# A sparse-attention mixer: one product for the compressed scores of both key groups, and keys, copies and low parts put in another order

## What is computed

```python
kc = apply_rope(rms_norm(compress(heads(k_cmp), pe_k, w1_k, w2_k), g_kc), ang_c[:, None])   # 2 groups x 15 keys x 64
vc = compress(heads(v_cmp), pe_v, w1_v, w2_v)
def block_fn(i):                                   # 128 queries at a time, 2 blocks
    m_c = cmp_end[None, :] <= tq[:, None]
    p_c = masked_softmax(jnp.einsum('bhgqd,bhnd->bhgqn', qb, kc) * scale, m_c)
    o_c = jnp.einsum('bhgqn,bhnd->bhgqd', p_c, vc)
    ...                                            # o_s: selected blocks, o_w: window
    return gb[..., 0:1] * o_c + gb[..., 1:2] * o_s + gb[..., 2:3] * o_w
```

## Time and profile before

| | us |
|---|---|
| median of 3 runs (1245.08 to 1246.0) | 1245.83 |
| the profiled execution | 1243.11 |
| its span | 1241.4 |
| PE busy | 1220.3 (98%) |
| DVE busy | 703.9 (57%) |
| ACT busy | 553.9 (45%) |
| mean granted TensorE clock, share of full | 0.99 |

### The profile page before, as it was taken

How to read it: one execution, slowest core, us unless ns; L and a number is a source line. 1 busy time by engine, 2 the same in 40 slices (tenths; PEclk the granted TensorE clock), 3 DMA queues, 4 the chain that set the end, 5 groups by cost and what they waited for, 6 DMA issues and landing times.

```text
span 1241.4 us, 14939 instructions
## 1 busy us (share of the span) xinstructions
PE 1220.3 (98%) x6235; PEld 1022.3 (82%) x6235; DVE 703.9 (57%) x714; ACT 553.9 (45%) x656; POOL 62.5 (5%) x121
## 2 busy tenths in 40 slices
PE   8999999999999999999999999999999997999998
PEld 6888888888889978888888888888888776888886
DVE  5667455455465755555546555546935776555452
ACT  5535344334355534543434534434656233444430
POOL 2100000000010001000000000002200010000000
PEclk9999999999999999999999999999999897999999
DMA  7754465656486327665546665545651314455550
GB/s 271 271 203 157 155 198 187 203 187 207 146 274 204 103 63 259 198 212 187 204 132 213 197 203 175 206 147 181 213 181 49 102 51 136 159 184 169 201 203 34
DMA packets 147700, 217.95 MB, mean 176 GB/s; under 512 B 5137, under 2 KB 115761, under 8 KB 147506
## 3 DMA queue, kind: packets, MB, share of 16 engines
q1 hardware_dynamic: 144658, 206.69, 50.4%
q0 software_dynamic: 2976, 10.31, 2.3%
HBM read 215.93 MB, written 1.05 MB: 175 GB/s over the span
## 4 chain that ended last, share of the span: by engine, by line
PE 95%; DVE 3%; ACT 1%; issue 1%; DMA 0%; POOL 0%; SPq 0%; DVEq 0%; POOLq 0%; ACTq 0%
PE acc L1734 28%; PE acc L1736 28%; PE acc L1735 28%; PE turn L1727 4%; PE acc L1937 1%; PE acc L2184 1%; DVE w_lo L1097 1%; PE turn L1862 1%; PE turn L2048 1%; PE turn L2162 1%; PE turn L1917 1%; DVE xt L1107 1%; DVE pt L1193 0%; PE turn L2133 0%; PE turn L2067 0%
## 5 line engine op out<-in xcount | busy, mean ns | idle before, releaser
L1097 DVE TENSOR_TENSOR w_lo<-raw,w_hi 128x2048 fp32r<-128x2048 f32 (+1 forms) x192 | 433.3, 2279 | 190.9 <-ACT w_hi L752 190.6
L1734 PE MATMUL acc<-w_hi,xt 128*128 128x512 f32 (+2 forms) x1112 | 436.5, 393 | 4.7 <-DVE xt L1107 2.5
L1736 PE MATMUL acc<-w_hi,xt 128*128 128x512 f32 (+2 forms) x1112 | 429.3, 386 | 0.0
L1735 PE MATMUL acc<-w_lo,xt 128*128 128x512 f32 (+2 forms) x1112 | 428.9, 386 | 0.0
L752 ACT ACTIVATE w_hi<-raw 128x2048 fp32r<-128x2048 f32 (+1 forms) x192 | 360.6, 1907 | 145.0 <-PE acc L1736 126.4
L1734 PEld LDWEIGHTS acc<-w_hi,xt 128*128 128x128 f32 x1112 | 210.7, 189 | 48.1 <-issue 2.8
L1736 PEld LDWEIGHTS acc<-w_hi,xt 128*128 128x128 f32 x1112 | 210.4, 189 | 42.7
L1735 PEld LDWEIGHTS acc<-w_lo,xt 128*128 128x128 f32 x1112 | 210.9, 190 | 39.4
L797 ACT ACTIVATE sg<-acc,rstd 128x256 f32<-128x256 f32 x88 | 37.0, 472 | 241.4 <-PE acc L1736 241.4
L1734 PE MATMUL acc<-w_hi,ht 128*128 128x512 f32 x352 | 139.1, 395 | 0.0
L1736 PE MATMUL acc<-w_hi,ht 128*128 128x512 f32 x352 | 138.2, 393 | 0.0
(11 more groups left out here) (263 smaller groups left out, 879.7 us busy)
## 6 DMA issues: line engine op xcount, KB each, us to landing
raw<-in_ffn_w_gate_up SPq DMA_DIRECT2D x88, 512.0 KB, 5.0
raw<-in_ffn_w_down SPq DMA_DIRECT2D x22, 1024.0 KB, 5.1
raw<-in_ffn_wg SPq DMA_DIRECT2D x44, 512.0 KB, 4.1
raw<-in_ffn_wu SPq DMA_DIRECT2D x44, 512.0 KB, 5.1
raw<-in_ffn_wd SPq DMA_DIRECT2D x22, 1024.0 KB, 5.2
raw<-in_a_w_in SPq DMA_DIRECT2D x15, 1024.0 KB, 6.6
raw<-in_w_in SPq DMA_DIRECT2D x10, 1024.0 KB, 5.2
raw<-in_a_w_out SPq DMA_DIRECT2D x8, 1024.0 KB, 5.8
```

Source lines behind the costliest of these rows:

```text
L1097: V.tensor_tensor(w_lo[:, u % RING, 0:kt * w], raw[:, u % RAW, 0:kt * w], w_hi[:, u % RING, 0:kt * w].bitcast(F32), ALU.subtract).then_inc ...
L1734: mm(o, lhs[0], rhs[0], start=start, stop=False)
L1735: mm(o, lhs[0], rhs[1], start=False, stop=False)
L1736: return mm(o, lhs[1], rhs[0], start=False, stop=stop)
```

## The change

- On PE, `compressed_scores` makes the scores of both groups with one product for each tile t and head index j: 8 products of 128 rows x 32 key columns in place of 16 products of 64 rows x 16. For this `kct` holds zeros where a row's group and a column's group differ. They fill one bank in place of two, so every later bank has a number lower by one.
- POOL zeroes `kct` once, before its mixer loads. DVE copies the turned keys in two pieces of 64 x 16.
- On DVE, the making of the keys moves ahead of `shift2(3)`, and the copy to `kct` (`turned_keys`) stands after `shares2(2)`, ahead of `part_out(1, 0)`.
- On DVE, the low parts of two `w_out` units, which were made in a row ahead of `compressed_scores`, are made singly: one there, one in `compressed_shares` ahead of the copy of `N_CP`. The last unit's low part moves behind `shares2(4)`.

```diff
-    N_CS = banks(2)
+    N_CS = banks(1)
...
             link(nc.gpsimd.memset(posi[:], 0))
+            link(nc.gpsimd.memset(kct[:], 0.0))
...
                 V.tensor_copy(kcn[:, 1, :], kcn[:, 0, :]).then_inc(s_ckn, 1)
-                copy_bank(N_CKT, kct[:], 32)
+
+            def turned_keys():
+
+                dve.wait_ge(s_turned, N_CKT + 1)
+                for g in range(2):
+                    rows, cols = slice(64 * g, 64 * g + 64), slice(16 * g, 16 * g + 16)
+                    last = V.tensor_copy(kct[rows, cols], tb[N_CKT % 4][rows, cols])
+                last.then_inc(s_tfree, 1)
 
             def compressed_scores():
+                dve.wait_ge(s_turned, N_CS + 1)
+                both = tb[N_CS % 4][:, 0:256].rearrange("p (t j g n) -> p g t j n", t=2, j=4, g=2)
                 for g in range(2):
-                    n = N_CS + g
-                    dve.wait_ge(s_turned, n + 1)
-                    V.tensor_tensor(shares[:, :, g],
-                                    tb[n % 4][:, 0:P].rearrange("p (t j n) -> p t j n", t=2, j=4),
-                                    spread(cmp_add[:], [[16, 2], [0, 4], [1, 16]]), ALU.add).then_inc(s_tfree, 1)
-                dve.wait_ge(*freed(N_CS + 1))
+                    last = V.tensor_tensor(shares[:, :, g], both[:, g], spread(cmp_add[:], [[16, 2], [0, 4], [1, 16]]), ALU.add)
+                last.then_inc(s_tfree, 1)
+                dve.wait_ge(*freed(N_CS))
...
+                split_to(U_MOUT + 3)
                 copy_bank(N_CP, cmp_st, 256)
...
             compressed_heads()
+            compressed_keys()
             shift2(3)
             shares2(2)
+            turned_keys()
             part_out(1, 0)
-            compressed_keys()
-            split_to(U_MOUT + 3)
+            split_to(U_MOUT + 2)
             compressed_scores()
             shift2(4)
             shares2(3)
             compressed_shares()
             shift2(5)
+            shares2(4)
             split_to(U_MOUT + 4)
-            shares2(4)
             compressed_out()
...
             def compressed_scores():
                 pe.wait_ge(*freed(N_CKT))
-                for g in range(2):
-                    b = take(N_CS + g)
-                    rows = slice(64 * g, 64 * g + 64)
-                    for t in range(TT):
-                        for j in range(4):
-                            c0 = 64 * t + 16 * j
-                            last = mm(b[:, c0:c0 + 16], z[rows, t, j * P:(j + 1) * P], kct[rows, 16 * g:16 * g + 16],
-                                      start=True, stop=True)
-                    last.then_inc(s_turned, 1)
+                b = take(N_CS)
+                for t in range(TT):
+                    for j in range(4):
+                        c0 = 32 * (4 * t + j)
+                        last = mm(b[:, c0:c0 + 32], z[:, t, j * P:(j + 1) * P], kct[:], start=True, stop=True)
+                last.then_inc(s_turned, 1)
```

## The result

| | before | changed | ratio (95% interval) |
|---|---|---|---|
| median with the first runs, us | 1245.45 (4 runs, 1242.7 to 1246.0) | 1237.7 (4 runs, 1237.47 to 1238.31) | 0.9950 (0.9937 to 0.9963) |
| again, beside e5, e7, e9 | 1244.84 (14 runs) | 1237.03 (6 runs) | 0.9933 (0.9918 to 0.9948) |
| again, beside e10, e12 | 1243.09 (9 runs) | 1236.98 (5 runs) | 0.9952 (0.9938 to 0.9965) |
| profiled execution, span | 1241.4 | 1236.6 | |

The changed kernel is faster by 0.5 to 0.7%, 6 to 8 us.

A forecast was written before the change was run, and what follows sets the result against it. TensorE, busy 98%, was taken to bound the kernel, with 10.2 us at half clock. Full-clock saving 7.5 us (wait 1.5, products about 1 to 2, rest clock) less 2.1 gave 1245.83 - 5.4 = 1240.4 us; range 1236.8 to 1243.9.

The forecast's parts named there:

- Keys ahead of the maxima: On DVE, keys end at 960.0, maxima start 1.26 us later; no cost on the path, PE's 1.54 us wait goes.
- Half the products: PE's compressed scores: 16 records over 128 rows take 1.93 us instead of 5.7, bounds 1.4 and 3.4.
- The sum at full clock: PE from the keys' transpose at 962.57: 9.2 us of work, `values2(3)` at 971.75 not 979.26, saving 7.5 us.
- B: Rival: clock falls near the small records' end, returns with wide ones, costing 2.1 us; saved 5.4, 1240.4 us; chance 0.41.
- A: Rival: the clock does not fall in this piece; full 7.5 us saved, 1238.3 us; chance 0.32.
- C: Rival: clock falls and stays low as long as before, 10.2 us; saved 2.4, 1243.4 us; chance 0.13.
- D: Rival: DVE late, PE waits, 1 to 2 us lost; chance 0.08. As length: PE's `scores2(3)` start to `values2(3)` start.
- What stood ahead of the fall: PE before 966.6: a 1.54 us wait, then narrow records; a busy engine alone did not keep the clock up.
- The saving passes to all behind it: PE's order and durations from `values2(3)` to the first nsa = 1 `mixed_tile` unchanged, 13.3 us, so all behind gains.
- Low parts one at a time: On DVE around the compressed scores' mask: dealing low parts out singly saves up to 1 us the faster PE would lose.
- The rest at nothing: POOL's memset, later mixer loads and renumbered banks cost nothing; thinnest cover 0.4 us, at `turn_shares2(4)`'s second bank.
- E: Rival: low clock, once taken, stays until long dense products; slower from a 20 us stretch, 1249 us; chance 0.06.

The follow-up runs named there:

- e5: Changed kernel with the compressed scores again as 16 products of 64 rows and 16 columns, both groups in turn, two banks: 1237.53 us, 0.9939 of before.
- e7: Changed kernel with the 16 records of the compressed scores streaming 128 columns each: 1236.69 us, 0.9932 of before.
- e9: Changed kernel with the 8 products of the compressed scores issued twice: 1239.96 us, 0.9966 of before.
- e10: e7 plus 14 filler products of 256 columns in the memory attention: 1234.91 us, 0.9931 of before.
- e12: e7 with the low parts as before, two in a row ahead of the mask: 1235.93 us, 0.9943 of before.
- e1: Kernel before with only the keys made ahead of the maxima, still 16 products of 64 rows: 1240.0 us, 0.9972 of before.
- e8: Changed kernel run again without any edit: 1237.03 us, 0.9933 of before.
- e11: Changed kernel run a third time without any edit: 1236.98 us, 0.9952 of before.
- e2: Kernel before with only the 8 merged products on zero-filled kct in one bank, DVE's order as before: 1240.32 us, 0.9974 of before.
- e3: Changed kernel with the low parts as before, two in a row ahead of the mask: 1236.93 us, 0.9950 of before.

## Why the prediction came out as it did

**Keys ahead of the maxima: right.** Keys from 958.67, maxima from 960.07, `kct` ready at 963.33 against 963.2 forecast, no PE wait for `pt` or `kct`. The wait of 1.54 us is gone.

**Half the products: right, and sized well.** 1.93 us taken, 1.85 measured. The bound of 1.4 did not come. The 64-row records at full clock are 0.10 to 0.11 apart in e1 and the merged ones 0.116; it was my halving of a spacing that is mostly at half clock (0.175 to 0.088) that was wrong. Sixteen more of them cost about 1.7 us, within the 1 to 2 given. The upper bound took 0.21 a record at half clock from a row that gives only roughly that (1.91 for 8 is 0.24), but e9 bears it out: its second 16 records took 3.4 us at half clock. The shorter time drawn from the Trainium skill, page "TensorE: Matmul & The Clock Gate", section "LDWEIGHTS", did not come either, though the rule itself, that a load's time does not go by its rows, comes near: 0.10 to 0.11 and 0.116.

**The sum at full clock: right in its mechanism, 0.4 us too long.** 14.5 us from 957.25 to 971.75 forecast, 14.1 in e8 and e11. The terms for the records of `values2(2)` (1.93, now 1.84), for the compressed scores (1.93, now 1.85) and for the transposes (0.9, now 0.79) were a little large. The full-clock saving in this piece is 22.0 - 14.1 = 7.9, not 7.5.

**The clock: both cases real, the wrong one called likelier.** B described the profiled execution closely: low from 966.58 to 969.98, 3.4 us, ended by wide records. A described the next two profiles of the same kernel. I gave B 0.41 and A 0.32 and had not said that one kernel can do both; the forecast of 1240.4 then stood for a single draw. B's price was 2.1, measured 1.6: the prediction had taken the middle between 1.7 and 2.5, and the stretch was the shorter one, 3.4 us, half of which is 1.7. With the terms as measured the local saving is 6.3 (B) to 7.9 (A), where 5.4 and 7.5 were forecast, and the medians moved by 6.1 to 7.8. The failed step is the weighing of small records: "more than the 2.85 that held" was read as speaking for a fall, and a fall came in one profile of three. The chances were also added up wrongly: by the prediction's own rule, A, B, half of C and most of D make about 0.85 for faster, not 0.81. That the profiled execution took 1238.31, only 0.6 from the 1237.7 forecast for it, is in part luck: this piece saved 6.3 where 5.4 were forecast, and 1.3 were lost behind it. The median fell by 7.8, what case A gives, though the profiled run beside it was B; the two later sets of runs moved by 7.8 and 6.1.

**What stood ahead of the fall: half right.** The reading that a busy engine alone does not keep the clock up stands, though the row at 971 that it cites is not all narrow records (the first wide scores began at 971.04): in the first profile of the changed kernel PE was busy for all 26.0 us from 957 to 983, and the clock fell at 966.58. The Trainium skill, page "TensorE: Matmul & The Clock Gate", section "Why this matters for your kernels", looks to idle gaps only; this trace shows a fall without one. The wait is not needed for a fall: e1 without it had 6.8 us of low clock, e2 with it 3.4. Whether it adds to one stays open, since a difference of 3.4 us is what one kernel shows between its profiles.

**The saving passes to all behind it: wrong by 1.3 us in the profiled pair.** The first `mixed_tile` with nsa = 1 came 6.05 us earlier (992.52 and 986.47), with 13.3 us from `values2(3)` to it in both, as forecast; the end came only 4.8 earlier. From there to the end the time was 248.88 before and 250.13 after. The work there is the same; the low clock from 1018 to 1050 was 17.1 in place of 13.7 us. Over all kernels without fillers the same distance is 248.7 to 248.9 with 13.7 us low and 249.9 to 250.6 with 17.1 us. Whether this holds for the medians is not shown. Runs of before differ in the same way: they go from 1240.21 us, with a mean granted clock of 0.992, to 1248.03 with 0.987, but only one of them has a trace.

**Low parts one at a time: right.** Up to 1 us was forecast for the faster PE; e12 against e7 gives 1.0 in D, and e3 against e8 and e11 1.0 to the end of the span.

**The rest at nothing: right.** `turn_on(0)` waits 0.51 against 0.48; the second bank of `turn_shares2(4)`, the thinnest cover, was met. Cases C, D and E did not occur.

## What to carry to other kernels

Small products at the end of a dependency chain cost more than their columns: a float32 record over 128 rows took 0.12 us here whether it had 32, 64 or 128 columns. And half clock began in or right behind a few microseconds of them in six of the thirteen profiles, and lasted into the wide work behind them; it did not come in the four profiles where the compressed scores had 128 or 256 columns, nor in e3, e8 and e11 with 32 columns, so the cause is likely but not proven. Merge them over zero-filled blocks, or take different rows of the array in turn, and make their inputs early, with the slack of the engine that makes them. When a change touches such a stretch, forecast a mixture of runs with and without the low clock, and judge it by many runs and by one distance in the trace, not by one span.

## What was not expected of the hardware

- The same program had 3.4 us of half clock behind the compressed scores in one profile and none there in two others, with no change in the order or the waits of PE. The start of the piece (`scores2(3)` at 957.46, 958.92 and 957.71) differed as well.
- The low clock in this piece lasted from 0 to 10.2 us, and the one from 1018 to 1050 from 13.6 to 17.1 us (3.4 with fillers), by kernel and by run.
- A float32 record over 128 rows costs 0.116 us with 32 columns, 0.121 with 128 and 0.225 with 256.
- Raising the clock of a stage that waits much gives back little: 13.7 us less at half clock in the memory attention, bought with 14 filler products, saved 2.1.
